# Pass 0 of the experts gathers rows of token tiles 0 to 6 by an early table; the rows of tile 7 are added in PSUM by products with a selection matrix

## The reference

```
h = h + m_lat[2] * y                                    # y: the mixer's output
v = modulate(rmsnorm(h, norm_ffn[l]), m_lat[3], m_lat[4])
...
lg = xt @ w_grp + b_grp;  p_g, grp = top_k(softmax(lg), 1)      # 4 groups
le = (xt @ w_exp + b_exp) of the chosen group; top_p, top_i = top_k(softmax(le), 2)
gate = p_g * top_p / sum(top_p);  expert = grp * 8 + top_i
...
y[token] += gate * ((silu(xb @ w1[e]) * (xb @ w3[e])) @ w2[e])   # xb: the rows of the tokens of expert e
```

## Time and profile before

| what | value |
|---|---|
| three runs | 2500.59, 2501.31, 2501.49 us, median 2501.31 us |
| the profiled execution: span from first to last instruction | 2494.6 us |
| what lies around the span, against the median | 6.7 us |
| TensorE busy | 2372.1 us, 95% of the span |
| VectorE, ScalarE, GpSimd busy | 1143.0, 361.5, 294.1 us |
| mean DMA rate over the span | 233 GB/s |
| transfers of the experts' weights | 384 of 1024 KB, 10.5 us from issue to landing in the median |

### The profile page before, as it was taken

One profiled execution on the slowest core, in us unless ns is written; L12 is line 12 of the kernel. 1 busy time (PEld: TensorE's weight loads), 2 busy tenths in 40 slices (PEclk: granted clock), 3 DMA queues, 4 the chain that ended last, 5 costly groups with the idle time before them and its releaser, 6 DMA issues. The chain is left out here.

```text
span 2494.6 us, 33367 instructions
## 1 busy us (share of the span) xinstructions
PE 2372.1 (95%) x14149; PEld 1058.1 (42%) x14150; DVE 1143.0 (46%) x2405; ACT 361.5 (14%) x645; POOL 294.1 (12%) x313
## 2 busy tenths in 40 slices
PE   4999999989999999999999899999999999999997
PEld 3545444544555523333233344444555333334433
DVE  1788377767945423322222544434455223322226
ACT  2310233331012200000000240000121000000002
POOL 2000000001000222122220000000002122221200
PEclk9999999999999999999999999999999999999999
DMA  9577100020170599999999611112106999999994
GB/s 307 200 251 275 34 26 26 17 110 34 68 286 34 213 357 402 402 404 413 388 409 410 240 34 51 34 51 85 76 29 254 378 406 402 414 402 414 406 379 202
DMA packets 140530, 581.41 MB, mean 233 GB/s; under 512 B 16756, under 2 KB 41640, under 8 KB 87768
## 3 DMA queue, kind: packets, MB, share of 16 engines
q1 hardware_dynamic: 120648, 534.87, 55.1%
q0 software_dynamic: 19648, 44.09, 4.8%
q10 hardware_dynamic: 80, 0.26, 0.0%
HBM read 550.74 MB, written 44.32 MB: 239 GB/s over the span
## 5 line engine op out<-in xcount | busy, mean ns | idle before, releaser
L1709 PE MATMUL ps<-arena 128*32 128x512 f32 x6144 | 678.9, 595 | 16.8 <-DMA arena<-in_ex_w_dram 16.8
L1709 PEld LDWEIGHTS ps<-arena 128*32 128x32 f32 x6144 | 207.2, 110 | 440.7 <-issue 423.7
L1744 PE MATMUL ps<-arena 128*32 128x512 f32 x3072 | 344.2, 598 | 11.2 <-DMA arena<-in_ex_w_dram 11.1
L1869 PE MATMUL ps<-arena 128*128 128x512 f32 x616 | 264.5, 592 | 0.0
L2497 DVE TENSOR_TENSOR arena<-arena,ps 128x512 f32<-128x512 f32 x48 | 52.3, 1090 | 456.2 <-PE ps L1709 456.2
L1589 PE MATMUL ps<-arena 128*128 128x512 f32 x512 | 229.4, 598 | 1.6 <-DVE arena L2273 1.6
L1744 PEld LDWEIGHTS ps<-arena 128*32 128x32 f32 x3072 | 119.1, 111 | 226.2 <-issue 207.5
L822 POOL DMA_INDIRECT arena<-normed_rows,arena x184 | 185.7, 1009 | 111.6 <-issue 52.5
L2542 DVE TENSOR_TENSOR arena<-ps,gates 128x512 f32<-128x512 f32 x96 | 61.8, 686 | 257.4 <-PE ps L1744 257.4
L1869 PEld LDWEIGHTS ps<-arena 128*128 128x128 f32 x616 | 117.0, 190 | 147.3 <-issue 147.3
L1402 PE MATMUL ps<-arena 128*128 128x512 f32 x384 | 167.3, 593 | 0.7 <-issue 0.7
(11 more groups left out here) (325 smaller groups left out, 2297.0 us busy)
## 6 DMA issues: line engine op xcount, KB each, us to landing
arena<-in_ex_w_dram SPq DMA_DIRECT2D x384, 1024.0 KB, 10.5
arena<-in_mod_w_dram SPq DMA_DIRECT2D x24, 2048.0 KB, 8.7
arena<-expert_rows SPq DMA_DIRECT2D x16, 1024.0 KB, 7.7
arena<-in_od_w_in_dram SPq DMA_DIRECT2D x12, 1024.0 KB, 5.4
arena<-in_x_dram SPq DMA_DIRECT2D x2, 4096.0 KB, 15.4
expert_rows<-gates SPq DMA_DIRECT2D x8, 1024.0 KB, 22.4
normed_rows<-arena POOLq DMA_DIRECT2D x16, 512.0 KB, 2.9
arena<-in_ev_w_in_dram SPq DMA_DIRECT2D x3, 2048.0 KB, 13.1
```

The lines of the kernel that those rows point to most:

```text
L1709: ins = nc.tensor.matmul(bank(2 + m)[c:c + n], x[:, j, c:c + n], w_slot(e % 2, m, KC, FE)[:, j], start=j == 0, stop=j == KC - 1)
L1744: ins = nc.tensor.matmul(bank(5 + half)[c:c + n], HT[:, j * P + c:j * P + c + n], w_slot(e % 2, 2, FC, D)[:, j, half * 512:(half + 1) * 51 ...
L1869: ins = nc.tensor.matmul(bank(4 * (g % 2) + b), x[:, j], y[:, j], start=first and j == 0, stop=j == 3, skip_group_check=True)
```

## The change

The table is read twice. After tile 6 (`table_of_rows(TT - 2)`, now ahead of the logits of tile 7) VectorE makes the token numbers of pass 0 alone, `EARLY_TOK`, and GpSimd gathers by them from the rows of tiles 0 to 6; slots that no token of these tiles has are skipped, so GpSimd clears the buffer XG first. Tile 7's part is made without DRAM: ScalarE scales tile 7 a second time into XC, in column order; VectorE's `select` makes a matrix SEL with a one where a token of tile 7 has a slot of pass 0; TensorE's `early_columns` (the old column products, moved out of `experts` and left open in PSUM) is followed by `last_tile_columns`, 8 matmuls XC x SEL that add to the same PSUM banks. Only then `x_T` goes up. VectorE scales its half of pass 0's columns ahead of the whole table's row numbers, and the 16 matmuls that spread the token numbers (`pieces`) now stand inside pass 0's first up product, after three of its eight chunks. GpSimd writes tile 7's rows behind the early gather. ScalarE takes both halves of tile 7's column copies. Of the spare matmuls, those after the turn of tile 7 become 2 of 4, those around the table and the spreading (4, 3 and 8) go, and 4 stand ahead of pass 0 in place of 5.

```
--- before
+++ after
@@ -248,6 +248,8 @@
...
         RHS = at(34592, 2, NJ * NE)
+        XC, SEL, SEL_SLOT = at(47104, D), at(48128, P), at(48256, 2)
+        EARLY_F, EARLY_ROW, EARLY_TOK = at(48258, 1), at(48259, 1).bitcast(I32), at(48260, 1).bitcast(I32)
         HOT0 = at(30720, 2, 7040)[:, :, 0:TT * P].rearrange("p k (t q) -> p k t q", t=TT)
@@ -815,8 +817,8 @@
...
                     pool.indirect_dma_start(
-                        XG[:, 0], None, rows_hn, bass.IndirectOffsetOnAxis(ap=PASS_TOK[:, 0:1], axis=0),
-                        bounds_check=SEQ - 1, oob_is_err=False).then_inc(x_full[0], 16)
+                        XG[:, 0], None, rows_hn[0:SEQ - P], bass.IndirectOffsetOnAxis(ap=EARLY_TOK, axis=0),
+                        bounds_check=SEQ - P - 1, oob_is_err=False).then_inc(x_full[0], 16)
                     return
@@ -837,14 +839,20 @@
...
             def experts(l):
-                for i in range(TT):
+                def rows_kept(i):
                     pool.wait_ge(xn_ready, norm_base[2 * l + 1] + i + 1)
...
 
-                for b in range(2):
-                    pool.wait_ge(hn_out[b], 16 * (TT // 2) * (l + 1))
+                for i in range(TT - 1):
+                    rows_kept(i)
+                pool.wait_ge(out_mm, 2 * TT * (l + 1))
+                step(nc.gpsimd.memset(XG[:, 0], 0.0), 3 + l + 1)
+                pool.wait_ge(hn_out[0], 16 * (TT // 2) * (l + 1))
+                pool.wait_ge(hn_out[1], 16 * ((TT // 2) * (l + 1) - 1))
                 pool.wait_ge(row_ready, 2 * l + 1)
                 gather(l, 0)
+                rows_kept(TT - 1)
+                pool.wait_ge(hn_out[1], 16 * (TT // 2) * (l + 1))
                 pool.wait_ge(row_ready, 2 * l + 2)
@@ -1154,6 +1162,10 @@
...
                     act.wait_ge(ms_ready, sb_ + 2 * i + 2)
+                    if i == TT - 1:
+                        nc.scalar.activation(XC.rearrange("t (c p) -> t c p", c=KC),
+                                             H[:, i].rearrange("t (p c) -> t c p", c=KC), ACT.Identity,
+                                             scale=rstd[:, i:i + 1])
                     nc.scalar.activation(XN[:, i % 2].rearrange("t (g c r) -> t g c r", g=4, c=KC),
@@ -1163,6 +1175,8 @@
...
                     nc.scalar.activation(VTT[:, i % 2, 512:], bank(5), ACT.Copy).then_inc(u_act, 1)
+                    if i == TT - 1:
+                        nc.scalar.activation(VTT[:, i % 2, 0:512], bank(4), ACT.Copy).then_inc(u_ready, 1)
 
@@ -1627,12 +1641,31 @@
...
                 def table_of_rows(i):
-                    pe.wait_ge(hot_ready, t0 + l + i + 1)
+                    pe.wait_ge(hot_ready, t0 + 2 * l + i + 1 + (i == TT - 1))
                     for k in range(2):
                         ins = nc.tensor.matmul(bank(7)[:, 0:NP], HOT0[:, k, i], RHS0[:, k, i],
-                                               start=i == 0 and k == 0, stop=i == TT - 1 and k == 1)
-                    if i == TT - 1:
+                                               start=i == 0 and k == 0, stop=i >= TT - 2 and k == 1,
+                                               skip_group_check=True)
+                    if i >= TT - 2:
                         ins.then_inc(tab_mm, 1)
+
+                def early_columns():
+                    pe.wait_ge(x_full[0], gathered(l, 0))
+                    pe.wait_ge(h_ready, 2 * TT * (l + 1))
+                    for j in range(KC):
+                        for g in range(4):
+                            nc.tensor.matmul(
+                                bank(j // 4)[32 * g:32 * g + 32, (j % 4) * P:(j % 4 + 1) * P],
+                                XG[:, 0, g * 256 + j * 32:g * 256 + j * 32 + 32], ident, start=j % 4 == 0, stop=False,
+                                skip_group_check=True)
+
+                def last_tile_columns():
+                    pe.wait_ge(hot_ready, t0 + 2 * l + TT)
+                    pe.wait_ge(xn_ready, nb + TT)
+                    for j in range(KC):
+                        ins = nc.tensor.matmul(bank(j // 4)[:, (j % 4) * P:(j % 4 + 1) * P], XC[:, j * P:(j + 1) * P], SEL,
+                                               start=False, stop=j % 4 == 3, skip_group_check=True)
+                    ins.then_inc(x_T, 1)
 
@@ -1647,22 +1680,15 @@
...
                 turn_rows(TT - 1)
-                spare(4, 2)
+                spare(2, 2)
+                table_of_rows(TT - 2)
                 logits(TT - 1)
-                table_of_rows(TT - 2)
                 spare(8, 2)
...
                 nc.tensor.matmul(bank(4)[:, 0:NE], ones, RUN[:, TT - 1], start=True, stop=True).then_inc(pos_mm, 1)
-                spare(4, 2)
+                early_columns()
+                last_tile_columns()
                 table_of_rows(TT - 1)
-                spare(3, 2)
-                pe.wait_ge(hot_ready, t0 + l + TT + 1)
-                for t in range(4):
-                    for g in range(4):
-                        ins = nc.tensor.matmul(bank(7)[32 * g:32 * g + 32, (4 + t) * NP:(5 + t) * NP],
-                                               ident[:, 32 * t:32 * t + 32], TOK_F, start=True, stop=True)
-                ins.then_inc(tab_mm, 1)
-                spare(8, 2)
 
@@ -1699,6 +1725,14 @@
...
                         pe.wait_ge(w_full[e % 2][m], (l * NE + e - e % 2 + 2) // 2 * 32)
+
+                def pieces():
+                    pe.wait_ge(hot_ready, (TT + 2) * (l + 1))
+                    for t in range(4):
+                        for g in range(4):
+                            ins = nc.tensor.matmul(bank(7)[32 * g:32 * g + 32, (4 + t) * NP:(5 + t) * NP],
+                                                   ident[:, 32 * t:32 * t + 32], TOK_F, start=True, stop=True)
+                    ins.then_inc(tab_mm, 1)
 
@@ -1710,6 +1744,8 @@
...
                             ins.then_inc(half_mm, 1)
+                        if p == 0 and m == 0 and j == 2:
+                            pieces()
                     return ins
@@ -1748,15 +1784,7 @@
...
 
-                pe.wait_ge(x_full[0], gathered(l, 0))
-                for j in range(KC):
-                    for g in range(4):
-                        ins = nc.tensor.matmul(
-                            bank(j // 4)[32 * g:32 * g + 32, (j % 4) * P:(j % 4 + 1) * P],
-                            XG[:, 0, g * 256 + j * 32:g * 256 + j * 32 + 32], ident, start=True, stop=True)
-                ins.then_inc(x_T, 1)
-                pe.wait_ge(h_ready, 2 * TT * (l + 1))
-                spare(5, 2)
+                spare(4, 2)
                 for p in range(NP):
@@ -2350,6 +2378,13 @@
...
 
+                def select(place_, slot):
+                    link(V.tensor_scalar(SEL_SLOT, place_, float(CAP), FAR, ALU.is_ge, ALU.mult))
+                    link(V.tensor_tensor(SEL_SLOT, SEL_SLOT, slot, ALU.add))
+                    link(V.tensor_scalar(SEL, cst[:, K_IOTA:K_IOTA + P], SEL_SLOT[:, 0:1], None, ALU.is_equal))
+                    V.scalar_tensor_tensor(out=SEL, in0=cst[:, K_IOTA:K_IOTA + P], scalar=SEL_SLOT[:, 1:2], in1=SEL,
+                                           op0=ALU.is_equal, op1=ALU.add).then_inc(hot_ready, 1)
+
                 def place(i):
@@ -2362,6 +2397,8 @@
...
                     link(V.tensor_tensor(slot, place_, first, ALU.add))
+                    if i == TT - 1:
+                        select(place_, slot)
                     shape = [P, 2, NP - 1]
@@ -2392,18 +2429,24 @@
...
                 mean_square(TT - 1)
-                columns_of(TT - 1)
                 scale(TT - 1)
+                dve.wait_ge(tab_mm, 3 * l + 1)
+                rows_out(bank(7)[:, 0:1], EARLY_F, EARLY_ROW, EARLY_TOK)
+                dve.sem_inc(row_ready, 1)
                 route(TT - 1)
...
                 place(TT - 1)
-                dve.wait_ge(tab_mm, 2 * l + 1)
+                dve.wait_ge(x_T, l * NP + 1)
+                for j in range(KC // 2):
+                    ins = V.tensor_scalar(XT[:, 0, j * P:(j + 1) * P], bank(0)[:, j * P:(j + 1) * P],
+                                          gain_x[:, n, j:j + 1], mod[:, l, 3, j:j + 1], ALU.mult, ALU.add)
+                ins.then_inc(xt_ready, 1)
+                dve.wait_ge(tab_mm, 3 * l + 2)
                 rows_out(bank(7)[:, 0:NP], PASS_F, PASS_ROW, PASS_TOK)
-                dve.sem_inc(row_ready, 1)
                 V.tensor_copy(TOK_F, PASS_TOK).then_inc(hot_ready, 1)
-                dve.wait_ge(tab_mm, 2 * l + 2)
+                dve.wait_ge(tab_mm, 3 * l + 3)
                 link(V.tensor_scalar(PIECE_F, bank(7)[:, 4 * NP:8 * NP], 4.0, QUARTER,
@@ -2500,14 +2543,6 @@
...
 
-                def first_x_cols():
-                    dve.wait_ge(x_T, n0 + 1)
-                    for j in range(KC // 2):
-                        ins = V.tensor_scalar(XT[:, 0, j * P:(j + 1) * P], bank(0)[:, j * P:(j + 1) * P],
-                                              gain_x[:, 2 * l + 1, j:j + 1], mod[:, l, 3, j:j + 1],
```

(5 more changed lines are left out.)

## The result

The kernel became a little slower: 2508.71 us in the median of five runs (2502.75 to 2512.87), against 2501.31 us (2499.04 to 2501.88) of the kernel before in the same comparison. The ratio is 1.0035, 95% interval 1.002 to 1.005. A second comparison with twelve runs gave 2507.04 against 2500.69 us, ratio 1.002 (1.0009 to 1.0032). The prediction was 2500.3 us, a little faster, with "within 0.2%" as the likeliest outcome; the time lies in its range, near the upper end, and the expected sign was wrong. The profiled execution took 2502.75 us with a span of 2500.9 us, against a span of 2494.6 us before.

A forecast was written before the change was run, and what follows sets the result against it. Each layer's end was set by when its first expert passes run, ahead of the weights' DMA stream. 2 x (-1.6 + 0.3) + 1.6 = -1.0 us; 2494.6 - 1.0 + 6.7 = 2500.3 us; range from near 2492.5 to 2509.1.

The forecast's parts named there:

- within 0.2%: Whole kernel: time between 2496.3 and 2506.3 us, not told from no change; chance 0.50.
- Landing, columns, tile 7's product, pass 0: Ahead of pass 0: rows at 847.3 + columns 3.4 + product 2.0 + 2.4 = 855.1, 5.2 us earlier.
- the fast landing: Early gather, ahead of pass 0: lands in 5.58 us as the old one, total 2492.5 us; chance 0.19.
- The second chain: Spreading, gathers (9.0 us later) and transposes for pass 1: pass 1 at 874.6, only 1.6 us of 5.2 left.
- One for one: Ahead of pass 0: any shift moves everything behind by as much, while the DMA still has holes.
- the stream swallows everything: Expert stage: the weights' stream absorbs the shift, no change, 2501.3 us; chance 0.08.
- I count one fall in two layers, at 1.6 us: TensorE's 3.4 us wait ahead of pass 1: clock falls in one of two layers, costing 8.66 - 7.07 = 1.6 us.
- 2 x 0.3 us: TensorE's 2.7 us idle time ahead of the columns: a clock fall priced at 0.3 us in each layer.
- the clock falls twice in both layers: Two idle times of TensorE per layer: falls cost 1.5 and 2.2 us, +4.2 in all, 2505.5 us; chance 0.12.
- The prediction's -1.0 us: Whole kernel: the summed change over both layers, 2 x (-1.6 + 0.3) + 1.6.
- all 6.7 us between the span and the median: Whole kernel: the median 2501.31 exceeds the profiled span 2494.6 by 6.7 us, taken to lie outside it and stay.

The follow-up runs named there:

- the kernel before with ten more increments: Kernel before, plus ten VectorE increments of a semaphore nobody waits for, in pass 6 of layer 1: 2502.85 us against 2500.2, ratio 1.0014.
- the version with both spares: Changed kernel plus eight spare products ahead of the columns, eight ahead of pass 0's hidden turn, and forty idle VectorE increments: 2497.4 us, ratio 0.9979 to before.
- the forty increments: Changed kernel plus forty VectorE increments of a semaphore nobody waits for, in pass 6 of layer 1: 2502.47 us, ratio 1.0016 to before.
- The spare products: Changed kernel plus eight spare matmuls ahead of the columns and eight ahead of pass 0's hidden turn: 2501.84 us; with forty idle VectorE increments too, 2497.4.

## Why the prediction was wrong

**Landing, columns, tile 7's product, pass 0.** Right, the columns in part by luck. Counted from the complete residual, pass 0 was to begin at 855.1 - 833.13 = 22.0 us, and began at 21.9. The early gather took 846.10 - 836.87 = 9.2 us to its use (8.6 + 0.9 predicted), the columns 3.6 us (3.4), the product 2.2 (2.0). The rival of the fast landing is out. But the 3.4 us of the columns were not their price at full clock. In the row they were taken from, the columns have idle times inside; the kernel before with ten more increments, the same program up to there, has them in 1.95 us in both layers, and pass 0 begins 25.8 and 25.0 us behind the residual where it began 27.2. Its layer 0:

```profile
853.93 1.95 PE L1754 MATMUL ps<-constants,arena 128*32 128x128 f32 x64 [1.82 <-DMA arena<-normed_rows,arena]
858.17 13.94 PE L1709 MATMUL ps<-arena 128*32 128x512 f32 x128
```

So the sum priced the columns nearly as if the clock had fallen, which it did, and it counted the gain from an execution of before whose pass 0 was 1.5 us late (2.2 us in layer 1).

**The second chain.** Right in kind and close in size. The gathers start at 858.59, 26.5 us behind the residual (27.8 predicted); from the fourth's start to the transposes are 867.94 - 862.58 = 5.4 us (4.4 taken, bounds 2.9 and 7.33); TensorE waited 4.36 us (3.4). Pass 1 was to begin 41.5 us behind the residual, and began at 873.63 - 832.07 = 41.6.

**One for one.** Right for delays, within the noise: +9.8 us for 9.5. For an earlier start it stays open how much arrives. In the version with both spares the turn of pass 0's hidden rows comes 2.8 and 4.5 us earlier against the residual than in the profile of before, 7.2 us in all, and the time is 4.1 us shorter; against the profile of before with ten more increments it is 1.3 and 2.3 us earlier, 3.6 in all. So between half and all of it arrives, depending on which profile of before one counts from. The rival that the stream swallows everything is out; that it swallows a part is not.

**The clock: the first step that failed.** "I count one fall in two layers, at 1.6 us". Behind the wait for the hidden product the clock fell in both layers, in all three profiles of the change (the second is its repetition, the third has the forty increments). From the first turn of hidden rows to the second are 23.6 and 23.0, 23.3 and 22.9, 23.5 and 23.0 us in the two layers, where before has 21.3 in both: 3.7 to 4.0 us in all, where the sum had 1.6. The wait was 4.36 us in layer 0 and 3.80 in layer 1, where the prediction had 3.4. Its 3.4 was 1.0 us short in layer 0 because the spreading was priced at 1.6 us of pass 0: the hidden product came where it was expected (39.4 us behind the residual, 39.7 predicted), but pass 0's products took 872.62 - 4.36 - 854.01 = 14.25 us and not 15.5.

Ahead of the columns the clock fell in both layers too, behind 4.14 and 3.47 us. That cost the sum nothing: 2 x 0.3 us stood for it by name, and another 2 x (3.41 - 1.95) = 2.9 us in the price of the columns. The spare products give back 5.2 us (without the forty increments) to 6.4 us (with them), each known within some 3 us; the sum had 1.6 + 0.6 + 2.9 = 5.1 us of it, named or not, so that the times alone would not show this step's error, and the profiles do.

The rule of the Trainium skill that the prediction weighed (TensorE: Matmul & The Clock Gate, HAM oscillation — how this bites in real kernels) says that a wait for DMA lets the next stretch start at half clock. Of the four waits, the two that end on a DMA are each followed by half clock; of the two that end on VectorE one is, and behind the other the clock fell only inside pass 1. The rule does not hold for every such wait: in the kernel before with ten more increments TensorE waited 3.63 us for weights and ran on at full clock.

```profile
2448.13 7.07 PE L1744 MATMUL ps<-arena 128*32 128x512 f32 x64 [3.63 <-DMA arena<-in_ex_w_dram]
```

The rival "the clock falls twice in both layers", 2505.5, was right in kind, and right in size behind pass 0 (2.2 us a layer against 2.3 and 1.7 to pass 1's turn). With 0.12 it had too small a chance, since the prediction read a bound for the fall between 3.06 and 3.79 us out of two rows, and put its own 3.4 beside it. That its total came so near is partly luck: its 1.5 us a layer ahead of pass 0 were not lost, as pass 0 began where the sum without them had it.

**The term that was missing.** No step spoke of the end of layer 1. The hole of 1.9 us on VectorE has nothing to do with what the change does, only with ten more instructions on VectorE. The prediction's -1.0 us becomes +1.4 us with the clock at the 4.0 us of the first profile, and +3.3 us with the length of the hole: the wrong sign is explained, and the second comparison's interval (2 to 8 us) holds this sum, the first's (5 to 12 us) does not. The rest, 3 to 4 us to the medians of 6.4 and 7.4, stays open. Two candidates stand in the traces and were not told apart: late sums that take 3 us longer in most profiles of the changed kernels, and the late pass 0 in the profile of before, from which the gain was counted.

**A reading without effect on the sum.** The prediction put all 6.7 us between the span and the median outside the span. In every execution of the comparisons 1.8 us lie outside it. The profiled execution of before was about 4.9 us faster than the median, and that of the change 6.0 us, so that the two profiles can be compared with each other, but a sum that starts from one of them cannot be read against a median to better than a few us.

## What to carry to other kernels

A change that takes a wait off TensorE and puts two shorter ones in its place can lose by the clock what it gains in time: list every idle time of TensorE that the change opens, and where the rows of before show the clock falling behind idle times about as long, price what follows at half clock in full. Before a duration is taken from a row of before, look for idle times inside it and at the clock it ran at: the columns' 3.41 us were 1.95 us of work. When a product releases the next chain of gathers, it belongs ahead of the wait, not behind the work: moving tile 7's table into the wait for the early rows was worth 11 us, in the version that also leaves out four spare products; that is more than the change itself. And read the whole timeline of the kernel after: a hole with no releaser, far from the change, can be a matter of where the instructions lie, which a few instructions that do nothing will test.

## What the runs showed of the hardware that was not expected

A queue of instructions (q14) moves packets of 8 KB while the kernel runs. In every profile one of them moves beside the last Else block of VectorE. In the six kernels whose block stands at instruction 3007 VectorE stood still for 1.8 to 2.1 us there, and in the eight whose block stands at 2997 or 3047 it did not. That VectorE waits for this packet is the reading that fits; the profile names no releaser.

The late sums of layer 1 took 27.73 us or 30.8 us behind idle times of the same 2.83 us, and a stretch behind 3.63 us of waiting stayed at full clock while one behind 2.08 us did not: at these lengths the clock fell in some executions and not in others.

A gather of 512 KB by row numbers, issued while the weights stream, took 9.2 us to its use, and one issued into emptier queues 5.58 us.
